# Second norm's rows through transposing transfers, third norm of four blocks on VectorE, gated operations ahead of sums: a streaming encoder step on eight cores

## The reference, cut to what matters

```python
z = x @ w_in                                   # u | v | gb | gc | xin, 512 each
a_out = u * (w_s-mix of layernorm(v) + b_s)    # over blocks of 128 positions
b_out = gb * (causal width-3 convolution of gc * xin)
x = layernorm(ALPHA * x + concat(a_out, b_out) @ w_out, ln_mix_g, ln_mix_b)   # norm 1
q = x @ w_q
x = layernorm(ALPHA * x + softmax(q k^T / 16) v @ w_mem_o, ln_mem_g, ln_mem_b) # norm 2
f = (silu(x @ w_gate) * (x @ w_up)) @ w_down
x = layernorm(ALPHA * x + f, ln_ffn_g, ln_ffn_b)                              # norm 3
```

## Time and profile before

| | |
|---|---|
| median of 3 runs | 3333.6 us (3333.21 to 3339.46) |
| profiled execution | 3339.72 us, of which the span of the slowest core (core 6) is 3338.2 us |
| spans of the 8 cores | 3286.8 to 3338.2 us |
| TensorE busy (core 6) | 3173.5 us, 95% |
| VectorE, ScalarE, GpSimd busy | 2370.2 (71%), 1476.6 (44%), 1051.5 us (31%) |
| transfers | 828 MB, mean 248 GB/s; SP's queue 75% of 16 engines |
| chain that ended last | PE 85%, DMA 5%, DVE 3%, issue 2%, ACT 2% |

### The profile page before, as it was taken

The page is one execution under the profiler, slowest core; times in us unless marked ns, Lnnn a source line. Parts: engine busy times, 40 slices in busy tenths (PEclk is TensorE's granted clock), DMA queues, the critical chain, the costliest instruction groups (busy, mean ns, idle before and its releaser), DMA issues.

```text
span 3338.2 us, 66412 instructions; the slowest of 8 cores (3286.8 to 3338.2 us)
## 1 busy us (share of the span) xinstructions
PE 3173.5 (95%) x20594; PEld 1891.3 (57%) x20594; DVE 2370.2 (71%) x4402; ACT 1476.6 (44%) x2720; POOL 1051.5 (31%) x914
## 2 busy tenths in 40 slices
PE   5977998999999999999999999999999999999996
PEld 2444443444457575756666575756666575756573
DVE  3665546667687777777787877777777877777763
ACT  4367542141345445354445344353545454353441
POOL 2010003012043432425253433425252433424253
PEclk8988998799999999999999999999999999999987
DMA  8976998779857786969787886969687777878674
GB/s 213 273 238 204 309 297 260 201 219 278 249 188 246 254 272 229 291 220 286 239 264 239 258 264 233 294 212 299 225 274 237 259 251 245 276 228 281 202 252 159
DMA packets 311717, 827.95 MB, mean 248 GB/s; under 512 B 27071, under 2 KB 104383, under 8 KB 311374
## 3 DMA queue, kind: packets, MB, share of 16 engines
q1 hardware_dynamic: 302078, 806.78, 75.3%
q0 software_dynamic: 9296, 16.91, 3.2%
HBM read 758.30 MB, written 82.19 MB: 252 GB/s over the span
## 4 chain that ended last, share of the span: by engine, by line
PE 85%; DMA 5%; DVE 3%; issue 2%; ACT 2%; SPq 2%; POOL 1%; DVEq 0%; POOLq 0%; ACTq 0%
PE bank L1348 26%; PE bank L1418 13%; PE bank L1056 13%; PE bank L1162 12%; PE bank L1268 6%; PE bank L1494 4%; PE bank L1117 3%; PE bank L651 3%; PE bank L1527 3%; DMA snap<-w_up 1%; DMA snap<-w_in 1%; DVE stg L943 1%; POOL small L1022 1%; DMA snap<-w_down 1%; DMA stg<-wscD 1%
## 5 line engine op out<-in xcount | busy, mean ns | idle before, releaser
L1022 POOL TENSOR_TENSOR small<-small 128x1 f32<-128x1 f32 (+1 forms) x195 | 229.1, 1180 | 837.9 <-DVE small L1020 740.6
L1056 PE MATMUL bank<-mring,mixT 128*128 128x512 bf16 x1920 | 480.9, 383 | 4.4 <-DMA mring<-wscM 2.5
L1162 PE MATMUL bank<-xT,mring 128*128 128x512 bf16 x1872 | 481.1, 384 | 0.0
L1301 POOL TENSOR_TENSOR hT<-snap,sg 128x512 f16<-128x512 f32 (+1 forms) x234 | 279.9, 1199 | 580.4 <-DVE sg L1297 409.2
L1354 ACT ACTIVATE snap<-bank 128x512 f32<-128x512 f32 (+1 forms) x468 | 257.0, 561 | 345.2 <-PE bank L1348 329.0
L1359 DVE TENSOR_TENSOR snap<-bank,snap 128x512 f32<-128x512 f32 (+1 forms) x468 | 296.5, 641 | 131.0 <-PE bank L1348 123.2
L1348 PE MATMUL bank<-x2T,fring 128*128 128x256 f16 x2560 | 328.0, 274 | 6.6 <-ACT mixT L654 2.8
L1056 PEld LDWEIGHTS bank<-mring,mixT 128*128 128x128 bf16 x1920 | 188.1, 99 | 196.3 <-issue 20.5
L1348 PEld LDWEIGHTS bank<-x2T,fring 128*128 128x128 f16 x2560 | 249.7, 98 | 81.1 <-issue 13.4
L1046 DVE SCALAR_TENSOR_TENSOR xres<-xres,bank 128x512 f32<-128x512 f32 x280 | 191.2, 683 | 143.2 <-PE bank L1056 125.5
L1008 ACT ACTIVATE x<-xres 128x1024 bf16<-128x1024 f32 (+1 forms) x128 | 134.7, 1053 | 349.4 <-DVE xres L1028 349.4
(11 more groups left out here) (288 smaller groups left out, 5261.5 us busy)
## 6 DMA issues: line engine op xcount, KB each, us to landing
mring<-wscM SPq DMA_DIRECT2D x322, 512.0 KB, 6.1
fring<-wscG SPq DMA_DIRECT2D x288, 512.0 KB, 6.8
stg<-wscG SPq DMA_DIRECT2D x215, 512.0 KB, 6.9
fring<-wscD SPq DMA_DIRECT2D x116, 512.0 KB, 5.0
stg<-wscD SPq DMA_DIRECT2D x89, 512.0 KB, 5.2
xres<-x_prompt SPq DMA_DIRECT2D x64, 512.0 KB, 9.5
y_prompt<-xres SPq DMA_DIRECT2D x64, 512.0 KB, 8.2
fring<-wscD SPq DMA_DIRECT2D x56, 384.0 KB, 4.7
```

Of the source, the lines that this page charges most:

```text
L1022: op("gpsimd", lambda e: e.tensor_tensor(out=m[0:SP, i, 3:4], in0=m[0:SP, i, 2:3], in1=mhalf[0:SP, 0:1], op=ALU.pow), 1.2, reads=[br, buf( ...
L1056: r = e.matmul(bk(L)[0:SP, :], lhsT=c.mixT[:, j * 4 + k, s * SP:(s + 1) * SP], rhs=t[:, k * 512:(k + 1) * 512], start=(j == 0 and k == 0), ...
L1162: r = e.matmul(bk(L)[:, 0:Tn], lhsT=tm[:, k * 256 + off:k * 256 + off + 128], rhs=c.xT[:, k, 0:Tn], start=(k == 0), stop=(k == 7))
L1301: op(eng, lambda e: e.tensor_tensor(out=dst, in0=Cu().rearrange("p (f t) -> p f t", f=n), in1=g.rearrange("p (f t) -> p f t", f=n), op=ALU ...
```

## The change

Three edits:
- In `ln_out`, norm 2 of prompt tiles 1 to 14 no longer uses `tr8`: SP issues one transfer from the `x16` buffer to `x2T` with `transpose=True`, which the planner counts as 786432 bytes. Norm 1, tile 0, the last tile (15) and the sample rows keep `tr8`.
- In `ln_tail`, norm 3 of tiles 0 and 1, of the last tile and of the sample rows is applied as norms 1 and 2 are, by two VectorE operations. Tiles 2 to 14 keep the old form.
- In `gated`, used by tiles 0, 1 and 2 and the sample rows, the three operations get keys smaller by 0.4.

```diff
         LK = 0.6
+        L3V = 2
 
@@ ln_out
-            tr8(x6, bxx, SP, idt, buf(ib), dst, db, "M", dt)
+            if c.smp or li == 0 or c.pos == 0 or c.last:
+                tr8(x6, bxx, SP, idt, buf(ib), dst, db, "M", dt)
+            else:
+                ld(lambda e: e.dma_start(out=dst, in_=x6, transpose=True), [bxx], db, "xtr%d" % ((xctr[0] - 1) % NX16), 786432)
@@ ln_tail
-            if li < 2:
+            if li < 2 or c.smp or c.last or c.pos < L3V:
...
-                if not defer:
+                if li < 2 and not defer:
                     ln_out(li, c, s)
                 return
@@ gated
+        PRG = 0.4
...
-            op("scalar", lambda e: e.activation(out=g, in_=bk(Lg)[:, 0:w], func=AF.Tanh), c_act(w), reads=[Lg], writes=[b])
+            op("scalar", lambda e: e.activation(out=g, in_=bk(Lg)[:, 0:w], func=AF.Tanh), c_act(w), reads=[Lg], writes=[b], dk=-PRG)
...
-               c_dve(w, True), reads=[Lg, b], writes=[b])
+               c_dve(w, True), reads=[Lg, b], writes=[b], dk=-PRG)
...
-               reads=[Lu, b], writes=hb)
+               reads=[Lu, b], writes=hb, dk=-PRG)
```

## The result

| | before | changed |
|---|---|---|
| median | 3335.84 us (3333.21 to 3339.46, 4 runs) | 3251.11 us (3243.61 to 3260.42, 4 runs) |
| profiled execution | 3339.72 us | 3243.61 us |
| spans of the 8 cores | 3286.8 to 3338.2 us | 3220.7 to 3241.8 us |

The ratio is 0.9747, with a 95% interval of 0.9719 to 0.9775: faster, by 84.7 us of the median. The forecast was 3268 us in a range of 3240 to 3345.

A forecast was written before the change was run, and what follows sets the result against it. TensorE was taken to bound the steady tiles, busy for all 50.00 us. Terms -21.1 + 6 - 12.4 - 13.4 - 25 = -65.9 us on span 3338.2 give 3272.3; + 1.5 - 6.1 makes 3268 us, range 3240 to 3345.

The forecast's parts named there:

- Transposes, -21.1: Norm 2, tiles 1 to 14: transposes leave TensorE, 0.44 us per row, 48 of 56 rows counted, -21.1 us.
- The charge, +6: Steady tiles: transposing transfers' queue time pushed into the saturated stretch, 0.5 us per tile, 12 tiles; ends 0 and +300 us.
- The nearer of the two rows: Price of a transposing transfer taken from the 256 KB `wscS` load, 3.4 us, not the 9.3 us casting load.
- Rival 2: Steady tiles: transfers too slow, deciding from 4.6 us per transfer; at 5.5 us the time is 3380 us; chance 0.19.
- latency condition: `x` buffers: a transfer may land about 9.5 us after its cast before ScalarE waits at the next cast.
- SP at nothing: SP's in-order queue: loads behind a transpose wait for its cast; seven ring slots cover it, priced at nothing.
- Tail, -12.4: Program end: norm 3 on VectorE instead of GpSimd ends at 3325.8 against 3338.2, -12.4 us; bounds -9 and -13.
- Hole, -13.4: Opening, 515 us: sums ahead of the gated operation; 11.7 us wait and 1.7 us half clock go; bounds -8, -15.
- Slow clock, -25: Opening, cores 6 and 7: the 0.81 stretch goes if the 515 us hole goes, -25 us; bounds 0 and -29.
- Rival 1: The slow clock stays or comes elsewhere: 3293 us; chance 0.22.
- low end: 3240 us: no transfer charge (-6), all 56 rows (-3.5), part of the end's slow clock won (118 us at 0.81 are 22).
- Rival 3: Transfers somewhat slow, 3.5 to 4.5 us each, 2 to 5 us per tile: about 3300 to 3325 us; chance 0.10.

The follow-up runs named there:

- e1: Changed kernel with all transposes of norm 2 back on TensorE and ScalarE: 3266.6 us, ratio 0.9808.
- e12: Changed kernel plus a plain 320 KB DRAM-to-DRAM copy ahead of each transposing transfer, holding no x buffer, compute orders kept: 3278.7 us, ratio 0.9857.
- e6: Changed kernel with each transposing transfer issued twice, same source and target: 3458.8 us, ratio 1.0408.
- e10: Changed kernel with tile 1's second norm transposed by TensorE too, transfers from tile 2 on: 3254.4 us, ratio 0.9785.
- e2: Changed kernel with the third norm of the last tile back on ScalarE and GpSimd: 3295.6 us, ratio 0.9844.
- e4: Changed kernel with the keys of the gated operations as before, norm 3 edit kept: 3304.3 us, ratio 0.9895.
- e3: Changed kernel with norm 3 of tiles 0, 1 and sample rows back on ScalarE and GpSimd, gated keys still lowered: 3286.4 us, ratio 0.9873.
- e5: Changed kernel with norm 3 of tiles 0 and 1 on GpSimd again and old gated keys: lowest 3309.2 us, median 3380.9, no ratio.
- e8: Changed kernel with the first norm's rows also transposed by transfers from tile 2 on: lowest 3251.0 us, ratio 0.9785.
- e9: Changed kernel with input rows also transposed by transfers from tile 2 on, norm 2's likewise from tile 2: 3258.4 us, ratio 0.9776.

## Why the prediction was right, and where it was not

The time lay in the range and on the right side, 17 us below the forecast. Against the profiled span the sum said -65.9 us and the trace says -96.4: 6.6 more in the opening, 8.8 more in the steady tiles, 15.1 more at the end.

**Transposes, -21.1: right in kind, too small.** e1 gives 24.0 us, and TensorE's busy time differs by 23.4 (2203.6 and 2180.1 us, core 3). The stretch holds 44 of the rows, not 48 (tile 3's are in the opening), so a row is worth 0.55 us and not the 0.44 read between two starts. The period of a tile before was 184.8 us and not 185.7.

**The charge, +6: nothing was paid in the steady tiles.** The nearer of the two rows was the right one to take: the transfers landed in 4.4 us. The step that failed is what the row was used for. Its landing time, 3.4 us, was taken for the time that a transfer occupies the queue, and that time is 1.8 to 1.9 us. By the prediction's rule the measured landing of 4.4 us would have cost 17.6 less 12.2 us per tile, about 65 us in all. The next step, that queue time pushed into a full stretch "starves one for one", does not stand either: with e12's copies the added queue time is about 14 us per tile, 1.8 over the 12.2 that were free, which should have cost some 20 us and cost 0.5, and TensorE stays at 10.00 in windows at 0.98 to 1.03. Loads that run ahead of their use would explain it; no run shows that by itself. Rival 2's threshold, 18 us per tile (4.6 per transfer), rests on these steps, and no run reached it without holding the buffers. The latency condition of the same part was the sensitive one: when two transfers leave each buffer back to back (e6), casts wait 129 us.

**SP at nothing: wrong in tile 1, and not by the step named.** "The loads behind a transpose wait for its cast" was written and priced at zero, with the ring slots as cover. In the steady tiles that held: SP waits 53.9 us for casts between 1000 and 3000 us, and TensorE has no wait for a transfer there. In tile 1 it was the issue itself that took 3.1 to 5.9 us in place of 1.22, with `w_down` pieces behind it that are still to be cast, and TensorE waits 5.1 us at 474. With tile 1's transposes back on TensorE (e10) the wait is gone and clean openings are 5 to 8 us shorter. The sum has no term for the length of an issue.

On both the Trainium skill had figures. "VectorE: DVE Perf Modes", "The three transpose paths", at 1309 ns for a block, gave 10.5 us per transfer; the trace has 1.8 to 1.9, so for a transfer of eight blocks this does not hold. Nor does the rule of the same page to stay on TensorE ("Rules for kernel authors"): staying costs 0.55 us of the bounding engine per row here. "Advanced Engine Details and Errata", "X-Bar Transpose (TRN2)", came nearer: from its sentence that they are as fast as regular transfers the prediction had a charge of zero. Its expected 350 to 400 GB/s would make 256 KB 0.7 us (an estimate from that page). The measured 1.8 to 1.9 us are about 140 GB/s, and the other transfers of SP's queue run at about 327 (547.7 MB in 75.6% of 2217.5 us, e1), so neither the rate nor the sentence holds here; that the steady tiles paid nothing did.

**Tail, -12.4: right.** e2 gives 11.9, the end of the changed kernel 17.7 us as forecast at about 17.

**Hole, -13.4: the wait went; the cause was half the story, and a second wait was missed.** The prediction held that GpSimd's passes slow the sums. They do (the passes themselves took 2.34 to 2.52 us beside them, against 2.34 at the shortest, so it is hardly mutual), but e4 has the sums at full speed with a hole of 14 us: VectorE's own norm passes take their place in the queue. It is the order that makes room for them (e3: 6 us left without the other edit). The clean opening of core 2 became 18.1 us shorter and that of the clean cores 24.6 in the mean, beyond the bound of -15; without the transfers (e1) it is 31.8. The forecast did not list the three waits at 633 to 639 us, 7.1 us, which went too, nor the new one at 474. Some 10 us of the 31.8 are not traced to a wait.

**Slow clock, -25: it came out so in this execution, but not by the reason given; this term was luck.** The changed kernel's profile has no stretch at 0.81, also not at the end, where the forecast left it; that is the 15.1 us missing there (153.3 less 137.8 before, 15.5). The step "if the hole is gone I expect the stretch to be gone" does not stand. In e3 all cores have the same 6 us hole and cores 2, 3, 6 and 7 go to 0.81 behind it while the others stay at 1.00; in e10 there is no hole at 500 and cores 2, 3, 6 and 7 run at 0.81 earlier, from 228 us; at the end a stretch of 102 to 117 us comes and goes between cores that execute the same instructions. Cores 2 and 4 of e3, from 550 to 700 us:

```profile
550.00:700.00 150.00, 149.20 (x621) 65.03 (x629) 85.65 (x153) 39.57 (x85) 8.15 (x15) 0.81 0.75 225
```

```profile
550.00:700.00 150.00, 149.29 (x768) 71.27 (x778) 106.25 (x188) 47.20 (x93) 17.72 (x22) 1.00 0.90 271
```

The stretches of before, e3, e5 and e10 in the opening begin behind a piece in which TensorE idled, as the one forecast on did. When such a piece is followed by a stretch, and when not, no run here explains. Rival 1 (the stretch stays or comes elsewhere) described e10 better than the changed kernel.

How much hangs on this can be read from the same kernel at other times. The kernel before, at 3333 to 3339 us in the comparison, also took 3298.0, 3300.2 and 3301.7 us beside the experiments, with no core under a mean clock of 0.980. The lowest of either kernel are 54 us apart (3298.0 and 3243.6), and the three stages of clean cores add up to 60.6 us (24.6, 24.0 and 12.0). The other 24 to 30 of the 84.7 us are a matter of which executions had a stretch, and no run shows that the change prevents one.

**In the range and the rivals.** The low end counts 22 us for the end's stretch, all of its 118 us at 0.81; e2 measured 15.6. Rival 3's 2 us per tile give 3268 - 6 + 24 = 3286 us and not 3300.

## What to carry to other kernels

- Moving work off the engine that bounds is worth its full time only where nothing of the new path is wanted soon: ask how long its source buffer is held, who is queued behind its issue, and which wait ends last once the engine is faster. The first move paid its full 24.0 us in the steady tiles and lost some 7 of them in the opening; the second and third (e8, e9) paid nothing.
- A hole with two causes has to be taken apart by removing each alone. Here one edit alone made it longer, the other halved it and took nearly all of the time back, and both together closed it.
- A transfer share near 1.00 is not a bound by itself, and the time to landing is not the time that a transfer takes of the queue. Load the queues with copies that nothing waits for, and look at whether the bounding engine notices.

## What was not expected of the hardware

**The 0.81 clock came in pairs of cores.** In every profiled execution here cores (0,1), (2,3), (4,5) and (6,7) had it together or not at all, stage by stage: before 6 and 7 in the opening and 4 to 7 at the end, e3 2, 3, 6, 7 in the opening and all but 4, 5 at the end, e8 0, 1, 6, 7 at the end, e12 6, 7 in the opening and 2, 3 at the end. The Trainium skill ("TensorE: Matmul & The Clock Gate", "Seeing it yourself") has the limit act on a whole die; these traces show pairs, and in the changed kernel all eight cores had TensorE busy for 99% of the steady tiles or more at a granted clock of 1.00. Pairs are what the profiles show and no rule: other executions have all four cores of a die low at once (e2, 3662.9 us: mean clocks of 0.853 to 0.862 on cores 4 to 7), as the page says. At the end a stretch of 102 to 117 us cost 14.4 us (139.9 less 125.5, e1) to 15.6 us (153.3 less 137.7, e2).

**One transposing transfer of 128x1024 fp16 within SBUF** took 1.22 us to issue in the median (1.7 to 7.2 for those of tile 1), 1.8 to 1.9 us of all 16 engines and 3.0 to 10.3 us to land. It added 1056 packets, (361214 - 302078) / 56, all under 512 bytes: 86207 against 27071 before.

**GpSimd's norm passes slow VectorE's sums.** An fp16 sum of 512 columns takes 0.42 us in the changed kernel, where no norm pass of GpSimd runs beside the sums, 1.33 in the mean beside its norm passes in e3 and up to 2.6.
